# Selective-scan kernel: the output product of group 6 runs block by block inside the chunks of group 7, which is written out

## What is computed

```python
z, xbc, dt = split(h @ in_w)                      # z gates, x, B, C go through a convolution
xbc = silu(conv(xbc)); xs, bm, cm = split(xbc)    # 8 groups, each 4 heads of 64, state 128
for each group, both directions, chunks of 128 tokens:
    states = einsum(B, to_end, x)                 # per chunk, then scanned over the chunks
    w      = (C . B) * decay * dt
    y      = w @ x + C . previous_state * exp(la_cum)
y   = (y + d_skip * x) * silu(z)
out = rmsnorm(y, norm_w) @ out_w                  # summed over the 8 groups
```

## Time and profile before

| | us |
|---|---|
| median of 3 runs | 2604.95 (2599.8 to 2607.89) |
| the profiled execution | 2605.17 |
| its span, first to last instruction | 2603.3 |
| PE busy | 2441.3 (94% of the span) |
| POOL busy | 1298.7 (50%) |
| DVE busy | 1446.5 (56%) |
| ACT busy | 805.6 (31%) |
| granted PE clock, mean | 0.966 |

### The profile page before, as it was taken

How to read it: one execution, slowest core, us unless ns; L and a number is a source line. 1 busy time by engine, 2 the same in 40 slices (tenths; PEclk the granted TensorE clock), 3 DMA queues, 4 the chain that set the end, 5 groups by cost and what they waited for, 6 DMA issues and landing times.

```text
span 2603.3 us, 36232 instructions
## 1 busy us (share of the span) xinstructions
PE 2441.3 (94%) x13506; PEld 2055.2 (79%) x13506; DVE 1446.5 (56%) x1785; ACT 805.6 (31%) x1724; POOL 1298.7 (50%) x1204
## 2 busy tenths in 40 slices
PE   7989999999999999999987999999999988998997
PEld 5767888888766788888876898898898887876786
DVE  7974211134776531111357688788788786227762
ACT  2343111112233420011233433333333432335771
POOL 6735766677774376666754234434444341362003
PEclk9999999999999999999988999999999997899999
DMA  4211344433221033444232111101101120121001
GB/s 154 81 49 49 121 138 138 140 120 105 85 77 65 33 113 129 139 138 130 97 104 81 33 49 42 55 32 48 48 32 48 48 97 27 33 81 49 1 2 49
DMA packets 33690, 199.30 MB, mean 77 GB/s; under 512 B 4400, under 2 KB 6576, under 8 KB 13616
## 3 DMA queue, kind: packets, MB, share of 16 engines
q1 hardware_dynamic: 22896, 159.93, 18.0%
q10 hardware_dynamic: 10688, 37.83, 4.4%
HBM read 192.50 MB, written 5.24 MB: 76 GB/s over the span
## 4 chain that ended last, share of the span: by engine, by line
PE 74%; DVE 16%; issue 5%; ACT 3%; POOL 1%; DMA 0%; DVEq 0%; ACTq 0%; SPq 0%; POOLq 0%
PE ps L407 36%; PE ps L697 11%; PE ps L934 5%; DVE convd L2069 3%; PE ps L815 2%; PE ps L515 2%; PE ps L793 1%; POOL wlo L363 1%; DVE xc L1770 1%; PE ps L832 1%; PE ps L1015 1%; PE ps L434 1%; PE ps L1032 1%; DVE convd L2083 1%; PE ps L624 1%
## 5 line engine op out<-in xcount | busy, mean ns | idle before, releaser
L359 POOL TENSOR_SCALAR whi<-wraw 128x512 fp32r<-128x512 f32 x584 | 399.8, 712 | 1260.9 <-PE ps L697 539.4
L363 POOL TENSOR_TENSOR wlo<-wraw,whi 128x512 fp32r<-128x512 f32 x584 | 869.3, 1518 | 0.0
L407 PE MATMUL ps<-uhi,whi 128*128 128x512 f32 x896 | 357.7, 399 | 24.5 <-DVE ulo L1721 18.1
L407 PE MATMUL ps<-uhi,wlo 128*128 128x512 f32 x896 | 351.2, 392 | 0.0
L407 PE MATMUL ps<-ulo,whi 128*128 128x512 f32 x896 | 350.5, 391 | 0.0
L697 PE MATMUL ps<-inhi,whi 128*128 128x384 f32 (+1 forms) x784 | 249.2, 353 | 24.8 <-ACT raw L1377 18.1
L697 PE MATMUL ps<-inlo,whi 128*128 128x384 f32 (+1 forms) x784 | 237.8, 338 | 0.0
L697 PE MATMUL ps<-inhi,wlo 128*128 128x384 f32 (+1 forms) x784 | 237.8, 338 | 0.0
L407 PEld LDWEIGHTS ps<-uhi,whi 128*128 128x128 f32 x896 | 169.6, 189 | 68.2 <-issue 24.9
L1890 DVE TENSOR_TENSOR h<-h,ps 128x1024 f32<-128x1024 f32 x40 | 48.8, 1221 | 307.8 <-PE ps L407 307.8
L407 PE MATMUL ps<-hidhi,whi 128*128 128x512 f32 x512 | 202.2, 395 | 0.0
(11 more groups left out here) (425 smaller groups left out, 4798.1 us busy)
## 6 DMA issues: line engine op xcount, KB each, us to landing
wraw<-in_wstream SPq DMA_DIRECT2D x150, 1024.0 KB, 4.8
modraw<-in_modw ACTq DMA_DIRECT2D x48, 512.0 KB, 3.5
hspill<-hres ACTq DMA_DIRECT2D x1, 3072.0 KB, 8.7
hback<-hspill ACTq DMA_DIRECT2D x1, 3072.0 KB, 9.8
h<-in_x ACTq DMA_DIRECT2D x2, 1024.0 KB, 5.0
out<-hfin SPq DMA_DIRECT2D x2, 1024.0 KB, 3.9
gw<-in_gates ACTq DMA_DIRECT2D x2, 512.0 KB, 5.2
pT<-in_pT ACTq DMA_DIRECT2D x2, 512.0 KB, 5.3
```

The lines of the kernel that those rows point to most:

```text
L359: pool.tensor_scalar(whi[:, s, c], wraw[:, s, c], 1.0, 0.0, ALU.mult, ALU.add).then_inc(wraw_read, 1)
L363: ins = pool.tensor_tensor(wlo[:, s, c], wraw[:, s, c], whi[:, s, c].bitcast(F32), ALU.subtract)
L407: mm = pe.matmul(ps[:, 2 * bank + m, :], a[:, w, c:c + P], b[:, kb, :], start=(n == 0 and i == 0), stop=(n == KB - 1 and i == 2))
```

## The change

- The loop runs over groups 0 to 5. Group 6 is written out with `defer=True`: on PE it ends after its last `next_half`, without its output product; on DVE its end has the convolutions, `squares` and `silu` without the eight `out_add` between them.
- The tiles of the last two groups come as z(6), x(7), bc(7), z(7), out(6), out(7): z(7) and out(6) have changed places, and with them the halves of `whi` and `wlo` in which they lie.
- In group 7 PE runs `former_block(2c)` and `former_block(2c+1)` in chunks c = 0 to 3, one ahead of and one behind `log_decay(c+1)`. A block has 12 matmuls of `uh`, `ul` of group 6 with out(6). They alternate between PSUM banks 0/1 and 2/3; block j from 2 on waits for the add of block j - 2 (`o_rd`).
- In group 7 DVE has `former_add(2c)` and `former_add(2c+1)` behind `weights(c+1)`, for c = 0 to 3.
- `uh` and `ul` of group 6 have to live through the first chunks of group 7, so that group 7 has an `xte_last` of its own for each chunk, in `raw` and `convd`; the ones of chunk 0 and 3 wait for transposes. ACT waits for tile out(6) to be done before it overwrites `uh`.

```diff
@@ tensor engine @@
+            def former_block(j):
+                if j == 0:
+                    wait_split(kt + 1)
+                    pe.wait_ge(z_rd, g * 2 + 1)
+                elif j == 1:
+                    pe.wait_ge(z_rd, g * 2 + 2)
+                else:
+                    pe.wait_ge(o_rd, g * 8 + j - 1)
+                dense((kt + 1) % 2, lambda i: i * D + j * P, P, U, range(2), j == KB - 1, 2 * (j % 2), None, None)
...
             for c, (name, part) in enumerate((("x0", 1), ("x1", 0), ("x1", 1), ("b", 0), ("b", 1), ("c", 0))):
-                next_half(name, part)
+                if last:
+                    if c < 4:
+                        former_block(2 * c)
+                else:
+                    next_half(name, part)
                 if c + 1 < NC:
                     log_decay(c + 1)
+                if last and c < 4:
+                    former_block(2 * c + 1)
                 y_part(c)
                 if c + 1 < NC:
                     off_part(c + 1)
             next_half("c", 1)
+            if defer:
+                return
...
-        with pe.Fori(0, GROUPS - 1) as g:
+        with pe.Fori(0, GROUPS - 2) as g:
             group(g, False)
+        group(GROUPS - 2, False, True)
         group(GROUPS - 1, True)
@@ vector engine @@
+                if last and c in (0, 3):
+                    dve.wait_ge(pre_ps, g * 6 + (6 if c else 4))
...
             offsets(2)
             weights(2)
+            former_add(2)
+            former_add(3)
...
+            elif defer:
+                conv(s1, 2, k)
+                conv(s1, 3, k)
+                silu(s1, 2)
+                squares(0)
+                squares(1)
+                silu(s1, 3)
@@ scalar engine @@
-            act.wait_ge(tile_done, kt + CREDIT)
+            act.wait_ge(tile_done, kt + CREDIT + (2 if last else 0))
@@ order of the tiles @@
-        tiles.append(out[g:g + 1])
+        if g == GROUPS - 1:
+            tiles.append(out[g - 1:g])
+        if g != GROUPS - 2:
+            tiles.append(out[g:g + 1])
```

More of the change, by code:

```diff
@@ L187, in build @@
     xte = at("xte", 147.375, [P, NC, 2, HPG, HD])
+    xte_last = [at(f"xte_last{c}", (135.125, 137.125, 139.125, 120, 122, 124)[c], [P, 2, HPG, HD]) for c in range(NC)]
     wdec = at("wdec", 184.375, [P, HPG, P])
@@ L792, in group @@
                         continue
+                    src = xte_last[c][:, d, :, :] if last else xte[:, c, d, :, :]
                     mm = pe.matmul(ps[:, 4 + (c + 2) % 4, d * 256:(d + 1) * 256], btok[:, c, :],
-                                   xte[:, c, d, :, :].rearrange("p r n -> p (r n)"), start=True, stop=True)
+                                   src.rearrange("p r n -> p (r n)"), start=True, stop=True)
                 mm.then_inc(st_ps, 1)
@@ L1492, in group @@
                 conv_tanh(s1, 3)
-        with act.Fori(0, GROUPS - 1) as g:
+        with act.Fori(0, GROUPS - 2) as g:
             group(g, False)
+        group(GROUPS - 2, False, True)
         group(GROUPS - 1, True)
@@ L2059, in conv_start @@
             dve.wait_ge(x_rd, s * 4 + (b + 1))
-            if not isinstance(s, int):
+            if not (isinstance(s, int) and s == 0):
                 dve.wait_ge(pre_ps, s * 6)
@@ L2212, in group, with out_add, former_add @@
             s1 = g + 1
+            blk = g * 10 + (3 if last else 5)
+            def out_add(j):
+                if j < KB - 1:
+                    dve.wait_ge(blk_ps, blk + j + 1)
+                else:
+                    done_wait(kt + (2 if last else 3))
+                q = OUT_BANK[j % 3]
+                V.tensor_tensor(halves(oacc[:, j, :]), halves(oacc[:, j, :]), ps[:, q:q + 2, 0:HALF], ALU.add
+                                ).then_inc(o_rd, 1)
+            def former_add(j):
+                if not last:
+                    return
+                if j < KB - 1:
+                    dve.wait_ge(blk_ps, g * 10 - 5 + 1 + j + 1)
+                else:
+                    done_wait(kt + 1)
+                q = 2 * (j % 2)
+                V.tensor_tensor(halves(oacc[:, j, :]), halves(oacc[:, j, :]), ps[:, q:q + 2, 0:HALF], ALU.add
+                                ).then_inc(o_rd, 1)
             skip(0)
@@ L2223, in group @@
             weights(1)
+            former_add(0)
+            former_add(1)
             if not last:
@@ L2238, in group @@
             weights(3)
+            former_add(4)
+            former_add(5)
             if not last:
@@ L2245, in group @@
             weights(4)
+            former_add(6)
+            former_add(7)
             if not last:
@@ L2320, in group @@
                 assert k.n == GROUP_STEPS, k.n
[L2322 removed]
+        with dve.Fori(0, GROUPS - 2) as g:
             group(g, False)
+        group(GROUPS - 2, False, True)
         group(GROUPS - 1, True)
```

55 lines of the change are left out of this document (23 added, 32 removed).

## The result

| | before, us | after, us |
|---|---|---|
| median of 5 runs each | 2605.13 (2599.8 to 2607.89) | 2621.98 (2620.69 to 2625.05) |
| the profiled execution | 2605.17 | 2620.69 |
| its span | 2603.3 | 2618.5 |
| granted PE clock, mean | 0.966 | 0.964 |
| from the second `silu` of group 6's end to the last one's end | 26.12 | 18.95 |

The ratio is 1.0068, with a 95% interval of 1.0053 to 1.0082: slower by 17 us. By the rows of the table the end of group 6 gains 7.2 us, the transposes lose 2.5, and group 7's chunks lose 25.7: the loss is in the chunks.

What follows compares the result with a forecast made beforehand. PE and DVE were taken as both full at group 6's end and as working in turns in group 7's chunks. The six terms sum to +18.5 us on 2605.17, forecasting a median of 2623.5 us, range 2611 to 2634.

Steps and rivals of the forecast that it cites:

- Term 1: End of group 6: without the output product and eight adds the last `silu` ends earlier, -8.4 us.
- Term 2: Group 7's transposes: after PE idles about 7 us they start at half clock, +2.2 us.
- Term 3: Chunk 0 of group 7: two blocks now stand between `off_part(0)` and `y_part(0)` on PE, +2.3 us.
- Term 4: Chunks 1 to 3: PE's block waits for an add behind `offsets` and `weights` on DVE, +12.0 us together.
- Term 5: Chunks 1 to 3: PE's idle time of about 4 us brings half clock, 2.2 us each, +6.6 us.
- Term 6: Chunk 4: POOL's split of A0 now falls on `offsets(4)` and `weights(4)`, +3.8 us.
- the transposes stay at half: Rival: group 7's transposes do not bring the full clock back; +21.3 us, 2626.3 us, chance 0.09.
- The chunks fill as in group 6: Rival: group 7's chunks 1 to 3 follow at PE's pace, 6.95 us each; kernel at 2599.7 us, chance 0.06.
- The clock stays up: Rival: the wait in chunks 1 to 3 is there without half clock; +7.8 us, 2612.8 us, chance 0.15.
- The clock at half throughout: Rival: half clock all through chunks 1 to 3, 6.8 us more in each; +32.3 us, 2637.3 us, chance 0.08.

Runs made afterwards that it cites:

- E1: The change with DVE's two adds of each chunk moved ahead of `gate_y`, nothing else altered: 2606.11 us, ratio 1.0003 to the kernel before.
- E3: The change with PE kept busy by unused matmuls, 34 ahead of group 7's transposes, 12 ahead of blocks 2, 4 and 6: 2616.88 us, ratio 1.0049 to before.
- E4: The kernel before with only group 6 written out behind the loop, no work moved: 2601.55 us, ratio 0.9984 to the kernel before.
- E5: The change without group 6's output product, its blocks and adds replaced by bare semaphore counts: 2602.11 us, ratio 0.9996 to the kernel before.
- E2: The change with DVE's two adds of each chunk between `offsets` and `weights`: 2617.55 us, ratio 1.0054 to the kernel before.
- E6: E1 with two blocks each in chunks 0 and 1, one each in 2 to 5, ACT's `uh` write behind `decays(5)`: 2595.22 us, ratio 0.9972 to before.
- E7: E6 with block 0 run ahead of group 7's transposes, its add first on DVE, bank pairs swapped: 2595.96 us, ratio 0.9974 to the kernel before.

## Why the prediction was right, and where its sizes were off

The forecast was 2623.5 us in a range of 2611 to 2634, the median is 2621.98. Its mechanism is what happened; its terms came out 2.5 us low, and what lies outside them made up for it. By its steps:

| step | forecast | measured, after against before |
|---|---|---|
| Term 1, end of group 6 | -8.4 | 26.12 to 18.95: -7.2 |
| Term 2, transposes after the idle time | +2.2 | 18.34 to 20.83: +2.5 |
| Term 3, chunk 0 | +2.3 | 4.00 to 6.47: +2.5 |
| Terms 4 and 5, chunks 1 to 3 | +18.6 | 20.12 to 40.02: +19.9 |
| Term 6, split of A0 on chunk 4 | +3.8 | 6.48 to 9.82: +3.3 |
| these together | +18.5 | +21.0 |

**Term 1** is 1.2 us too large a gain, in two places. The contention of DVE with the split fell on the taps as forecast: six of the eight are slow, three at about 1.25 us and three at about 1.92, and the two behind the end of the split (2097.53 on POOL) take 1.02 each; without a split a tap takes 1.05. But the sum had the two starts of the convolution (L2090, L2065 before) at their old price, and the second one took twice as long, 0.8 us more. After, then before:

```profile
2087.09 5.79 DVE L2094 SCALAR_TENSOR_TENSOR convd<-raw,cpg,convd 128x770 f32<-128x770 f32 x4
2092.80 1.65 DVE L2090 TENSOR_SCALAR convd<-raw,cpg 128x770 f32<-128x770 f32 x1
2094.49 5.97 DVE L2094 SCALAR_TENSOR_TENSOR convd<-raw,cpg,convd 128x770 f32<-128x770 f32 x4
```

```profile
2098.94 0.81 DVE L2065 TENSOR_SCALAR convd<-raw,cpg 128x770 f32<-128x770 f32 x1
```

And it took the eight adds with all the idle time beside them, 8.3 us, though the rows of DVE overlap by some 0.1 us each: from one start to the next an add took 0.87 us, so that less came free. Before, four of the eight adds stood beside the first split, and they took 0.95 us all through the earlier trace rows, beside it and after it. The Trainium skill has a rule for this, in SBUF — State Buffer, section Who interferes with whom: a DVE instruction with two inputs in SBUF contends with a GpSimd one that reads SBUF, one with a single SBUF input does not, outside the modes that use both ports. The trace agrees for these: the taps are slowed after, the squares before (3.33 us against 1.95), and the adds, with one input in PSUM, are not. The starts have one input in SBUF and are slowed as well; no run here shows in which mode they ran.

**Term 2** was right in size and cause. PE ran the transposes cold after 8.5 us (7 were forecast):

```profile
2104.20:2110.00 5.80, 5.73 (x27) 5.76 (x28) 2.84 (x7) 3.60 (x11) 0.00 (x0) 0.50 0.00 0
2110.00:2112.00 2.00, 2.00 (x13) 1.85 (x12) 2.00 (x5) 1.87 (x7) 0.00 (x0) 0.96 0.00 0
```

Until 2110.3 PE ran only transposes (L761 to L763), and the clock was back at 2110.1. So the rival *the transposes stay at half* falls. It had a rule of the Trainium skill behind it (TensorE: Matmul & The Clock Gate, Part 4: PE-mode transpose, that the full clock does not engage for them); in this trace it did. The size is partly chance: E1 waits as long (8.53 us) and comes to 19.91 us from the first transpose to `off_part(0)`, after takes 20.62 and before 18.13. Over the first 6.2 us of the transposes the mean clock was 0.64 in E1 and 0.53 after.

**Term 3** had the two blocks at their full length, and so they were.

**Term 4** was right in the instruction that waits, in what it waits for, and in size: 3.4 to 3.9 us where 3.3 to 4 was named. The sum of the steps at full clock was 10.7 us a chunk, and E3's chunks at full clock take 10.26, 11.19 and 11.15. In chunks 2 and 3 the sum had left out 0.4 us between PE's `off_part` and DVE's `offsets`: from start to start it is 1.17 us (2144.08 to 2145.25), and 0.78 was put. In chunk 1 the microsecond put on `weights(1)` for a split didn't come, as the split ended at 2132.94, before it. E1 shows that the wait is DVE's order and not the banks or the product: only the adds moved, and the kernel is back at 1.0003.

**Term 5** was put at 2.2 us a chunk, from a row with a wait of 2.2 us and one of 3.87. By E3 it is 2.5, three times. It had leaned to the row with the shorter wait; at 3.9 us the cost lay a little towards the other.

**Term 6** was taken from the same five instructions beside a split in group 6 (6.7 us); they took 6.9. Of the 4.0 us that they took longer, 3.3 reached the chunk's length: the chunk of before that it is compared with ran its `off_part` at half clock, 2.1 us from its start to that of `offsets(4)` where after has 1.2.

**Outside these terms** the sum had nothing, and three things happened. First, from `y_part(5)` to `residual` it took 1.0 us more, 15.79 against 14.78. It goes with the clock in all seven traces that can be compared: the longer PE stays at half behind `y_part(5)`, the later `residual` comes. Over the 6 us from `y_part(5)` on the mean clock was 0.72 in the kernel before, E1, E3 and E4, which take 14.75 to 14.78 us; 0.63 in E5, which takes 15.23; 0.53 after; and 0.51 in E2, which takes 15.85. (E6 and E7 have the split of A0 there.) Before, then after:

```profile
2169.30:2175.30 6.00, 6.00 (x30) 5.56 (x31) 4.40 (x8) 2.49 (x3) 0.00 (x0) 0.72 0.00 0
```

```profile
2186.40:2192.40 6.00, 6.00 (x25) 5.34 (x26) 3.75 (x7) 2.49 (x3) 0.00 (x0) 0.53 0.00 0
```

Second, the column sums at the end took 3.0 us less, also a gain from the clock: after the same wait of PE for DVE it was at half for 3.0 us in place of 6.0, and the one-column matmuls behind it then ran 7.1 us at 0.98 in place of 3.7 at 0.96. From that wait's end to PE's next transposes it is 23.06 us in place of 26.04. Before, then after:

```profile
2191.20:2197.20 6.00, 5.98 (x19) 5.98 (x20) 5.89 (x8) 0.00 (x0) 0.00 (x0) 0.50 0.00 0
2197.20:2200.90 3.70, 3.70 (x31) 3.70 (x29) 3.60 (x6) 0.84 (x1) 2.23 (x4) 0.96 0.00 0
```

```profile
2209.30:2212.30 3.00, 2.99 (x9) 2.99 (x10) 2.96 (x4) 0.00 (x0) 0.00 (x0) 0.50 0.00 0
2212.30:2219.40 7.10, 7.10 (x56) 7.10 (x55) 6.93 (x9) 1.84 (x3) 3.96 (x5) 0.98 0.01 2
```

E2, E6 and E7 show the same 3.0 us, E1, E3, E4 and E5 don't, and the code there is the same in all. Third, the second `silu` of group 6 came 4.0 us earlier (2085.11 against 2089.07), of which 3.7 lie ahead of the scan, where nothing differs (its first `z_gate` at 1445.66 against 1449.35; over the traces of all nine kernels it is anywhere from 1444.8 to 1451.8). So 21.0 + 1.0 - 3.0 - 4.0 makes 15.0 of the 15.2 us between the spans; the medians differ by 16.9. That the forecast is within 1.5 us of the median is partly luck, of these opposite signs: its terms were 2.5 us short where the change acts.

**The rivals.** *The chunks fill as in group 6* put its whole case on whether the add is over before `off_part(c)` ends. It wasn't, for the reason given against it; E1 is this rival made true, at 7.0 us a chunk where 6.95 was worked out. It came to 2606 and not to 2600 because of what that case left out: in E1 the cold transposes cost 1.8 us (19.91 against 18.13 from the first of them to `off_part(0)`) and the split of A0 3.3, and the end of group 6 gains 1.2 less. *The clock stays up* is E3, whose adds are in the change's places: 2616.9, not 2612.8, since that case had the split of A0 at half its price (1.9 us for 3.3) and Term 1's gain in full (1.2 us), and chunks 1 to 3 came to 12.5 us over before, not 12.0. *The clock at half throughout* fell: 0.73 to 0.75 in these chunks.

**What stays open**: why and where writing group 6 out gains some 4 us (E4), and so how much of the change's own result that gain hides; what sets whether a wait of about 2.6 us costs the clock, and how long half clock lasts after the same wait; and whether moving group 6's product is worth anything beyond writing the group out, which the times of E6 and E4 don't settle.

## What to carry to other kernels

When work is put into an engine's idle time, look up not only where it runs but where its consumer stands in the other engine's order. The consumer of a filler belongs ahead of the instruction that waits for the filler's engine, because behind it the two engines take turns: here that place alone was worth 0.65% (1.0068 against 1.0003), some 17 us. Then fill evenly and only to the length of the chain: a chunk with one block took 5.1 us, one with none 6.6 (at a clock of 0.76) and one with two 7.0 (PE full), and spreading the blocks took the kernel from 1.0003 to 0.9972. And ask what the end of each tile starts: here the split that it released took `offsets(4)` and `weights(4)` from 2.9 to 6.9 us.

## What was not expected of the hardware

- One wait of 2.57 us left the clock at 1.00 over its chunk, and the next wait of 2.57 us, after a chunk of the same instructions, came with 0.73 and 2.9 us more (E2).
- Transposes alone brought the clock back from 0.50 to 1.00, 5.8 us after they began.
- A chunk with more work in it was shorter than the same chunk with less: 5.1 us with a block of 12 matmuls (E6), 6.6 without (before), 7.0 without and with a wait of 2.5 us in it (E5).
- The same code after the same wait of PE (the last output blocks of the scan) was cold for 3.0 us in one kernel and 6.0 in another, which moved the end by 3.0 us.
- The same wait of 8.5 us left the transposes behind it at a mean clock of 0.53 in one kernel (after) and 0.64 in another (E1).
